# A decoder step on one core: the query's norm behind its product, compact sample attention, softmax in halves, memory keys split up

## The reference

```python
def rms_norm(x, g):
    y = x * rsqrt(mean(x * x) + 1e-5)
    return y * g

# memory of the prompt: m = rms_norm(mem, g_mem); k = m @ w_mk; v = m @ w_mv
def cross_attn(h, mk, mv, w_q, w_o):          # h = rms_norm(x, g_xattn)
    q = (h @ w_q)                             # 4 heads of 256
    s = einsum('bthd,bmhd->bhtm', q, mk) / 16
    pr = softmax(s)
    o = einsum('bhtm,bmhd->bthd', pr, mv)
    return o @ w_o
```

## Time and profile before

| | us |
|---|---|
| median of three runs | 1353.83 (1351.83 to 1354.12) |
| the profiled execution | 1351.44 |
| its span, from first to last instruction | 1349.6 |
| PE busy | 1281.6 (95%) |
| DVE busy | 401.5 (30%) |
| ACT busy | 197.1 (15%) |
| bytes moved | 464.25 MB, 344 GB/s on the mean |

### The profile page before, as it was taken

The page is one execution under the profiler, slowest core; times in us unless marked ns, Lnnn a source line. Parts: engine busy times, 40 slices in busy tenths (PEclk is TensorE's granted clock), DMA queues, the critical chain, the costliest instruction groups (busy, mean ns, idle before and its releaser), DMA issues.

```text
span 1349.6 us, 18887 instructions
## 1 busy us (share of the span) xinstructions
PE 1281.6 (95%) x8190; PEld 639.9 (47%) x8190; DVE 401.5 (30%) x799; ACT 197.1 (15%) x355; POOL 16.1 (1%) x39
## 2 busy tenths in 40 slices
PE   7999999999899999999999999999999999999995
PEld 5777865667575434344343433334333333433332
DVE  2998524520313121312212212121221212122112
ACT  3015232320312100001001010000100000010002
POOL 0002000000000000000000000000000000000000
PEclk9999999989999999999999999999999999999999
DMA  7435411294795999999999999999999999999995
GB/s 248 135 129 109 147 35 63 102 369 154 315 401 224 428 414 430 427 428 426 428 429 428 428 429 428 428 429 429 429 428 429 428 428 429 428 428 428 428 427 206
DMA packets 40280, 464.25 MB, mean 344 GB/s; under 512 B 8528, under 2 KB 10128, under 8 KB 12064
## 3 DMA queue, kind: packets, MB, share of 16 engines
q1 hardware_dynamic: 39392, 459.53, 82.2%
q0 software_dynamic: 832, 3.90, 1.0%
HBM read 458.34 MB, written 5.07 MB: 343 GB/s over the span
## 4 chain that ended last, share of the span: by engine, by line
PE 71%; DMA 26%; ACT 2%; DVE 1%; issue 1%; SPq 0%; DVEq 0%
PE ps L1086 32%; PE ps L560 27%; DMA arena<-in_w_gate 13%; DMA ring<-in_w_gate 10%; PE ps L1154 4%; DMA ring<-in_w_down 2%; PE ps L1110 2%; PE ps L1097 2%; PE ps L1103 1%; PE ps L1188 1%; PE ps L1144 1%; PE ps L1115 1%; ACT arena L1230 1%; DMA xT<-in_xT 0%; PE ps L1156 0%
## 5 line engine op out<-in xcount | busy, mean ns | idle before, releaser
L1086 PE MATMUL ps<-ring,xT 128*64 128x512 f32 x1536 | 342.7, 596 | 8.3 <-DMA ring<-in_w_up 5.6
L560 PE MATMUL ps<-arena,ring 128*128 128x288 f32 (+2 forms) x1152 | 233.0, 373 | 3.6 <-DVE arena L1466 3.1
L1086 PEld LDWEIGHTS ps<-ring,xT 128*64 128x64 f32 x1536 | 105.9, 137 | 235.2 <-issue 208.1
L560 PEld LDWEIGHTS ps<-arena,ring 128*128 128x128 f32 (+1 forms) x1152 | 181.2, 177 | 50.9 <-issue 8.7
L1086 PE MATMUL ps<-ring,arena 128*64 128x512 f32 x768 | 171.7, 596 | 10.3 <-DMA ring<-in_w_down 10.3
L1230 ACT ACTIVATE arena<-ps 64x512 f32<-64x512 f32 (+9 forms) x140 | 81.5, 589 | 642.5 <-PE ps L1103 331.0
L1086 PE MATMUL ps<-arena,xT 128*64 128x512 f32 x512 | 115.4, 595 | 3.1 <-DMA arena<-in_w_gate 3.1
L1086 PEld LDWEIGHTS ps<-ring,arena 128*64 128x64 f32 x768 | 53.2, 137 | 111.5 <-issue 97.4
L1878 DVE TENSOR_SCALAR xT<-ps 128x512 f32<-128x512 f32 x32 | 22.1, 692 | 184.3 <-PE ps L1086 184.3
L1086 PEld LDWEIGHTS ps<-arena,xT 128*64 128x64 f32 x512 | 35.6, 137 | 74.4 <-issue 66.8
L1833 DVE TENSOR_TENSOR xT<-ps,vec 128x1024 f32<-128x1024 f32 x15 | 18.4, 1225 | 172.8 <-PE ps L1115 172.8
(11 more groups left out here) (212 smaller groups left out, 782.0 us busy)
## 6 DMA issues: line engine op xcount, KB each, us to landing
ring<-in_w_up SPq DMA_DIRECT2D x64, 2048.0 KB, 31.9
ring<-in_w_down SPq DMA_DIRECT2D x47, 2048.0 KB, 31.5
ring<-in_w_gate SPq DMA_DIRECT2D x32, 2048.0 KB, 34.2
arena<-in_w_gate SPq DMA_DIRECT2D x32, 2048.0 KB, 33.7
arena<-in_w_down SPq DMA_DIRECT2D x16, 2048.0 KB, 34.8
ring<-in_w_in SPq DMA_DIRECT2D x4, 2048.0 KB, 7.9
ring<-in_cache_k SPq DMA_DIRECT2D x4, 2048.0 KB, 17.7
ring<-in_cache_v SPq DMA_DIRECT2D x4, 2048.0 KB, 8.8
```

What stands on the lines that cost most here:

```text
L560: return nc.tensor.matmul(out, lhsT, rhs, start=start, stop=stop)
L1086: last = nc.tensor.matmul(out[AT[h ^ swap], :], lhs(k), part(weights(i), 0, 4, D)[:, k % 4, h * 512:(h + 1) * 512], start=(fresh and k == ...
```

## The change

- Memory keys. Pieces 0 and 1 go ahead of the products that sum the squares of `kk`; pieces 2 to 11 behind them; pieces 12 to 15 go one behind each of the first four levels of the inversion. Blocks 6 and 7 use bank 7.
- The norm of q. DVE multiplies x by the gain alone, block by block right behind `xres`; `w_q` runs on that, and DVE multiplies each block of the result by `rs` while it empties the bank. The sum of squares stands behind the first block of `w_q`, in bank 7.
- Samples. DVE clears 2304 columns and copies the samples' queries into them, so that for sample b the operand of 32 tokens is zero except for its own four (`q_alone`). The products of all samples then accumulate in one region of 256 columns. The mask is gone and the softmax has 256 columns. Two transposes take the place of 16, and ACT spreads their result into another cleared area (`p_alone`), whose operands for the value products are zero outside their sample.
- The prompt's softmax is done in two halves of two heads, maximum, exponential, division (eight instructions of DVE), transposes and copies; ACT copies the first half of the turned probabilities, DVE the second.
- The prompt's outputs are made one head at a time (`attended`): two before the value products of the samples, one behind them, one behind the last turn. `w_o` waits for the last head only at its seventh product.
- Slot 6 waits for the samples' value products and slot 7 for the fourth head; the sums of squares for the router write four groups of rows where they wrote two.

```diff
-        ssam = part(arena, 10752, NB, MEM)
-        ssamT = part(arena, 2304, 2 * NB, P)
+        probs = part(arena, 13056, 8, MEM)
+        probsT = part(arena, 15104, 2, 2, 4 * P)
+        osam = part(arena, 17152, MEM)
+        ssam = arena[:, 17408:17664]
...
+        def q_alone(k, b):
+
+            return arena[:, 10752 + k * 288 + b * 32:10752 + k * 288 + b * 32 + 32]
+
+        def p_alone(m, b, h):
+
+            return arena[:, (m * XH + h) * 288 + b * 32:(m * XH + h) * 288 + b * 32 + 32]
...
-            last_front = [("wo_ps", 4), ("wo_ps", 8)] + [("sv_ps", n + 1) for n in range(4)] + [("o_out", 1), ("o_out", 1)]
+            last_front = [("wo_ps", 4), ("wo_ps", 8)] + [("sv_ps", n + 1) for n in range(4)] + [("sv_ps", 4), ("o_out", XH)]
...
+                        if ready and first + m == 0 and k in ready:
+                            pe.wait_ge(*ready[k])
...
-            pe.wait_ge(S["sq_done"], 3)
-            for c in range(CT):
-                take(4 + c)
-                last = mm(ps[:, 4 + c, 0:TW], mean64, tmp[:, c, :])
-                readers[4 + c] = [("kk_max", 1)]
-            last.then_inc(S["sum_ps"], 1)
...
-                    b = m % 4
+                    b = m % 4 if m < 6 else 7
...
-            for i in range(16):
+            mem_piece(0)
+            mem_piece(1)
+            pe.wait_ge(S["sq_done"], 3)
+            for c in range(CT):
+                take(4 + c)
+                last = mm(ps[:, 4 + c, 0:TW], mean64, tmp[:, c, :])
+                readers[4 + c] = [("kk_max", 1)]
+            last.then_inc(S["sum_ps"], 1)
+            for i in range(2, 12):
...
+                if l < 4:
+                    mem_piece(12 + l)
             mem_piece(16 + len(LEVELS))
...
-            take(0)
-            for k in range(KT):
-                pe.wait_ge(S["sq_done"], 7 + k)
-                last = mm(ps[:, 0, 0:TOK], ones, xsq[:, k, :], k == 0, k == KT - 1)
-            last.then_inc(S["sum_ps"], 1)
-            readers[0] = [("root", 7)]
+            def x_squares():
+                take(7)
+                for k in range(KT):
+                    pe.wait_ge(S["sq_done"], 7 + k)
+                    last = mm(ps[:, 7, 0:TOK], ones, xsq[:, k, :], k == 0, k == KT - 1)
+                last.then_inc(S["sum_ps"], 1)
+                readers[7] = [("root", 7)]
+
             for n in range(2):
-                linear("w_q", n, hT, TOK, range(8), "q_ps", 4 * n, lambda m: ("q_out", m + 1), steps=("h_done", 2 * KT + 1))
+                linear("w_q", n, hT, TOK, range(8), "q_ps", 4 * n, lambda m: ("q_out", m + 1), steps=("h_done", 2 * KT + 1),
+                       after=lambda m: None if m else x_squares())
             pe.wait_ge(S["q_out"], 8)
             take(*range(8))
 
-            for u in range(8):
-                h, t = u // 2, u % 2
-                for k in range(2):
-                    last = mm(ps[:, h, t * MEM:(t + 1) * MEM], q[:, 2 * h + k, t * P:(t + 1) * P], memK[:, 2 * h + k, :], k == 0, k == 1)
-            last.then_inc(S["s_ps"], 1)
-
+            for h in range(XH):
+                for t in range(2):
+                    for k in range(2):
+                        last = mm(ps[:, h, t * MEM:(t + 1) * MEM], q[:, 2 * h + k, t * P:(t + 1) * P], memK[:, 2 * h + k, :], k == 0, k == 1)
+                if h % 2:
+                    last.then_inc(S["s_ps"], 1)
+
+            pe.wait_ge(S["q_out"], KT + 1)
...
-                            last = mm(ps[32 * h:32 * h + 32, 4 + n, b * MEM:(b + 1) * MEM], q[:, 2 * h + k, SEQ:TOK],
-                                      keys[:, b, 2 * h + k, :], k == 0, k == 1)
+                            last = mm(ps[32 * h:32 * h + 32, 4, 0:MEM], q_alone(2 * h + k, 2 * n + b),
+                                      keys[:, b, 2 * h + k, :], n == 0 and b == 0 and k == 0, n == 3 and b == 1 and k == 1)
                 last.then_inc(S["sk_ps"], 1)
-            pe.wait_ge(S["s_norm"], 1)
-            for t in range(2):
+            for half_ in range(2):
+                pe.wait_ge(S["s_norm"], 4 * half_ + 4)
                 for m in range(2):
-                    for h in range(XH):
-                        last = nc.tensor.transpose(ps[:, 2 * m + t, h * P:(h + 1) * P], probs[:, 2 * h + t, m * P:(m + 1) * P], ident)
-            last.then_inc(S["pt_ps"], 1)
-            pe.wait_ge(S["pt_out"], 1)
-            for h in range(XH):
+                    for h in range(2):
+                        for t in range(2):
+                            last = nc.tensor.transpose(ps[:, 2 * half_ + m, (2 * h + t) * P:(2 * h + t + 1) * P],
+                                                       probs[:, 4 * half_ + 2 * h + t, m * P:(m + 1) * P], ident)
+                last.then_inc(S["pt_ps"], 1)
+
+            def attended(h):
+                pe.wait_ge(*((S["pt_out"], 1) if h < 2 else (S["s_norm"], 9)))
                 for d in range(2):
                     for m in range(2):
-                        last = mm(ps[:, h, d * SEQ:(d + 1) * SEQ].rearrange("p (t a) -> p t a", t=2), memV[:, m, (2 * h + d) * P:(2 * h + d + 1) * P],
-                                  probsT.rearrange("p m (t h) a -> p m h t a", t=2)[:, m, h, :, :], m == 0, m == 1)
-            last.then_inc(S["o_ps"], 1)
+                        last = mm(ps[:, h, d * SEQ:(d + 1) * SEQ], memV[:, m, (2 * h + d) * P:(2 * h + d + 1) * P],
+                                  probsT[:, h // 2, m, h % 2 * SEQ:(h % 2 + 1) * SEQ], m == 0, m == 1)
+                last.then_inc(S["o_ps"], 1)
+
             pe.wait_ge(S["ss_norm"], 1)
-            for j in range(2 * NB):
-                last = nc.tensor.transpose(ps[:, 4 + j // 4, (j % 4) * P:(j % 4 + 1) * P],
-                                           ssam.rearrange("p b m -> p (b m)")[:, j * P:(j + 1) * P], ident)
+            for m in range(2):
+                last = nc.tensor.transpose(ps[:, 5, m * P:(m + 1) * P], ssam[:, m * P:(m + 1) * P], ident)
             last.then_inc(S["st2_ps"], 1)
+            attended(0)
+            attended(1)
...
-                        last = mm(ps[32 * h:32 * h + 32, 4, 0:MEM], ssamT[:, 4 * n + j, 32 * h:32 * h + 32],
+                        last = mm(ps[32 * h:32 * h + 32, 6, 0:MEM], p_alone(j % 2, 2 * n + j // 2, h),
                                   vals[:, j // 2, j % 2, h * MEM:(h + 1) * MEM], n == 0 and j == 0, n == 3 and j == 3)
                 last.then_inc(S["sv_ps"], 1)
+            attended(2)
             pe.wait_ge(S["so_out"], 1)
             for d in range(2):
-                last = nc.tensor.transpose(ps[:, 5, d * P:(d + 1) * P], osam[:, d * P:(d + 1) * P], ident)
+                last = nc.tensor.transpose(ps[:, 7, d * P:(d + 1) * P], osam[:, d * P:(d + 1) * P], ident)
             last.then_inc(S["so_ps"], 1)
-            pe.wait_ge(S["o_out"], 1)
+            attended(3)
+            pe.wait_ge(S["o_out"], 3)
...
-                for d in range(2):
+                for d in range(4):
...
-                linear("w_o", n, mix, TOK, range(6), "wo_ps", 4 * n, lambda m: ("xres2", m + 1),
+                linear("w_o", n, mix, TOK, range(6), "wo_ps", 4 * n, lambda m: ("xres2", m + 1), ready={6: (S["o_out"], XH)},
...
-            for m in range(KT):
+            for m in range(6):
...
+                if l == 1:
+                    mem_key(6)
                 if l == len(LEVELS) - 2:
                     mem_value(0)
+                    mem_key(7)
...
-            inv_root((S["sum_ps"], 11), rs[:, :], ps[:, 0, 0:TOK], 1.0 / D, 0)
-            for m in range(KT):
-                act.wait_ge(S["q_ps"], m + 1)
-                tell("q_out", copy(q[:, m, :], ps[:, m, 0:TOK]), False)
-
-            act.wait_ge(S["s_max"], 1)
-            for u in range(8):
-                tell("s_exp", a.activation(probs[:, u, :], ps[:, u // 2, (u % 2) * MEM:(u % 2 + 1) * MEM], ACT.Exp,
-                                           scale=1.0 / 16, bias=amax[:, u:u + 1], accum_out=asum[:, u:u + 1]), False)
+            inv_root((S["sum_ps"], 11), rs[:, :], ps[:, 7, 0:TOK], 1.0 / D, 0)
+            for half_ in range(2):
+                act.wait_ge(S["s_max"], half_ + 1)
+                for u in range(4 * half_, 4 * half_ + 4):
+                    tell("s_exp", a.activation(probs[:, u, :], ps[:, u // 2, (u % 2) * MEM:(u % 2 + 1) * MEM], ACT.Exp,
+                                               scale=1.0 / 16, bias=amax[:, u:u + 1], accum_out=asum[:, u:u + 1]), False)
+            act.wait_ge(S["ss_max"], 1)
+            tell("ss_exp", a.activation(ssam, ps[:, 4, 0:MEM], ACT.Exp, scale=1.0 / 16, bias=amax[:, 8:9], accum_out=asum[:, 8:9]), False)
             act.wait_ge(S["pt_ps"], 1)
-            tell("pt_out", copy(probsT.rearrange("p m u a -> p (m u a)"), ps[:, 0:4, :].rearrange("p b f -> p (b f)")), False)
-            act.wait_ge(S["ss_max"], 1)
-            tell("ss_exp", a.activation(ssam, ssam, ACT.Exp, scale=1.0 / 16, bias=amax[:, 8:9], accum_out=asum[:, 8:9]), False)
-            act.wait_ge(S["o_ps"], 1)
```

(58 more changed lines are left out.)

9 lines of the change are left out of this document (3 added, 6 removed).

## The result

The changed kernel takes 1334.39 us (median of four runs, 1333.15 to 1335.5) and the kernel before, beside it, 1352.83. The ratio is 0.9866, with a 95% interval of 0.9853 to 0.9878. That is 18.4 us; forecast were 15.9 of gain and 1337.9 us, with 1334.5 to 1342.5 as the range, so the median lies 0.1 us under its lower end. The kernel before had medians of 1350.96 to 1352.14 us beside the later experiments, so the 18.4 are good to some 2 us. The profiled execution took 1333.15 us with a span of 1331.4, where that of before had 1349.6, so 18.2 us are to be found in the two traces.

The account below looks back on a forecast made before the run. The experts' loads set the end, but start with PE's first expert product, so front gains pass through. 6.2 + 8.3 + 1.6 - 0.2 = 15.9 us off the median of 1353.83 gave 1337.9 us, range 1334.5 to 1342.5.

Parts of the forecast that it names:

- The loads set the end, and it follows PE's first expert product: Experts: loads restart with PE's first product, so front gains reach the end one for one while 10 us of standstill exist.
- The norm behind the product, 6.2 us: Ahead of and in `w_q`: gain of 3.06 us idle time and 3.2 us of half clock.
- Attention, 8.3 us: End of samples' scores to `w_o`: 25.5 us become 17.1; bounds 7.3 and 8.6, 8.3 taken.
- Memory keys, 1.6 us: Keys, `prep` and inversion: earlier start less pieces given back, plus half of two stalls; bounds 0.3 and 2.8 us.
- the 0.55 us of the sum: Memory keys: what is left of the 7.5 us earlier start after the inversion's four pieces give back 6.95.
- The clearings cost nothing: DVE's two clearings of 2304 columns, 1.45 to 2.6 us each, were to be hidden beside other work.
- The router's sums, -0.2 us: Two sums of squares write four groups of rows, 4 more short records each: a loss of 0.2 us.
- the fourth rival: Samples' states land late behind SP's queue at the eighth key, PE waits in `sample_old`; slower, 1359 at 228 us; 3%.
- The rival of the stalls that stay: Inversion: the two stalls remain, belonging to a count of instructions and not their density; 1339.0 us, 15%.
- the third: Rival at the experts: standstill gone, loads bound by their own start, front's gain not passed on; 1352 to 1354, 4%.
- late handovers: Rival in the attention: ACT and DVE hand over late, about 1 us each, three make 1340.9 us; 9%.
- late states: Rival at SP's queue: samples' states land late and PE waits in `sample_old`; slower than before, 3%.

Follow-up runs that it names:

- w_o_half: Changed kernel with four of the eight products of each block of `w_o` left out, so its result is not the reference's; 1324.44 us.
- before_again: The kernel before, unchanged, run again for a second profile; 1349.52 us.
- norm_undone: Changed kernel with the sum of squares ahead of `w_q` again and the norm applied to x; 1340.74 us by the median.
- busy_wait: Kernel before with six unused products more in PE's idle time ahead of `w_q`; 1351.87 us beside 1351.99, ratio 0.9996.
- attention_alone: Changed kernel with the keys and norm parts both undone, leaving the attention part; 1341.72 us beside 1352.14 for the kernel before, ratio 0.9921.
- keys_fourteen: Changed kernel with fourteen pieces of the memory keys ahead of `prep` and only two in the inversion; 1338.94 us in five runs.

## Why the prediction was right

The mechanism, the order of the parts and the end came out as told; the size was 2.5 us short by the medians.

- *The loads set the end, and it follows PE's first expert product.* Shown: 928.5 us from that product to the end in both kernels, and the thirteen traces agree within 1.5 us. w_o_half marks the limit. 16.3 us less of front gave 8 to 10, about the standstill of 8 us that the changed kernel has left.
- *The norm behind the product, 6.2 us.* The stretch gave 6.19, but its working had two halves of which only one always holds. The idle time is worth 3.2 us: the kernel before at full clock (before_again) takes 38.97 us from the end of `w_out` at 289.40 to the scores at 328.37, the changed one 35.73 from 286.76, which is 290.64 less the first block's 3.88. The other 3 us were the half clock of this one execution. I took a row of one profile for a fixed cost; before_again, norm_undone and attention_alone have the same idle time and no fall behind it. As a premise that step failed, and that the number fitted the trace is luck. How often the fall comes stays open: norm_undone lost the full 6.3 us by its median, of which its trace at full clock explains 3.24 and some 0.8 for the wait on bank 7, while filling the idle time in busy_wait gained nothing.
- *Attention, 8.3 us.* 8.74. From the end of the samples' scores to `w_o` it is 16.8 us where I counted 17.1; PE waits under 0.1 us at each handover. The compact samples seem to bring most: halves 1.8 and heads apart 1.3 us were measured by undoing each, so 5.7 of the 8.7 are left for the transposes, the mask and the 2048-column softmax; that share is a remainder, if the three add up, and was not run by itself.
- *Memory keys, 1.6 us.* 3.15, above my own upper bound of 2.8. `prep` came 0.06 us later where I had 0.2, PE's wait there was 0.92 for 0.8. The term that failed is the stalls: I counted two of 2.1 us together, of which half should go, and both went; the third, 0.92 us at 150 us, I left out of the sum because no piece lies near it. It is a block of code behind `w_mv`, and the change moves that load. With the 0.55 us of the sum and 2.6 us for all three stalls less the 0.41 that is left, the working gives the 3.15.
- *The clearings cost nothing.* 1.98 us each, between my bounds of 1.45 and 2.6 and under the prediction's estimate of 2.4, and a whole further pair hides too.
- *The router's sums, -0.2 us.* 0.07 us of gain over `w_o` and the choice of experts; the added records vanish between the others.

Three sums of mine were off without touching the forecast: the parts' lower bounds give a gain of 13.6 us and not 13.4, the lower end of the range, 1334.5, has no term behind it below 1335, and the fourth rival's 228 us would give 1361.6 by its own terms and not 1359. The norm had no bounds at all, and the attention's 8.74 lies just above its 8.6.

The rival of the stalls that stay (1339.0) is refuted by the trace, the third by the 928.5 us. Those of late handovers and late states too: the states are issued at 186.55 us and PE doesn't wait in the recurrence. But keys_fourteen shows that the fourth rival looked at the wrong victim. In that run it is not PE's operand that a badly placed load delays but PE's own instructions.

Of the 2.3 us by which the traces differ more than forecast, 1.5 are the keys, 0.4 the attention and 0.3 the router. Against the medians stands another account. At full clock the parts come to 3.15 + 3.24 + 8.74 + 0.07 = 15.2 us, and the medians differ by 18.4. The kernel before has single runs with a mean granted clock from 0.991 to 0.997, and its slowest, 1356.43 us, is the one at 0.991; the changed kernel's four have 0.996 to 0.998. Six single runs of the kernel before at 0.997 took 1349.69 to 1351.12 us, and the changed kernel's three at 0.997 or 0.998 took 1333.15 to 1335.03: at like clocks the gain is 14.7 to 18.0 us, which holds the 15.2. In the three profiles with the old attention the clock fell once, once and three times in the front, three of these in the attention's waits. In eleven with the new attention it fell in three, at 398.7 and 398.4 us and behind the 4.62 us stall. That the change also removes places where the clock can fall, and that this is most of the other 3 us, fits. It was not isolated, and the counts are small; attention_alone, with 10.4 us by the medians and 8.74 in the trace, is too uncertain to tell.

## What to carry to other kernels

Where transfers set the end, ask how long they stand still ahead of the stage: up to about that many microseconds an earlier start pays in full, and beyond them, as w_o_half shows, not. When a load is moved past dense code, look at whether the engine's own instructions must come through at that time; idle times "issue" that lie whole multiples of 256 instructions apart give it away. A clock that fell in one profile is not a cost that every execution pays: price the idle time, and take a second profile for the rest.
